# A decoder trunk on eight cores: the gate of the first mixer folded into its output weights on Pool, chunks read a tile later, one weight cast a tile

## What is computed

```python
mod = (c_act @ ada_w[i] + ada_b[i])[:, None, :]          # (B,1,6D)
sh_m, sc_m, gt_m, sh_f, sc_f, gt_f = jnp.split(mod, N_MOD, axis=-1)
h = x * (1 + sc_m) + sh_m
...
return o.reshape(B, S, Q_WIDTH) @ w_o + b_o
...
x = layer_norm(DEEPNORM_ALPHA * x + (1 + gt_m) * y, post_ln_g[i, 0], post_ln_b[i, 0])
```

## Time and profile before

| | |
|---|---|
| time, median of 3 runs | 2449.65 us (2434.49 to 2452.31) |
| the profiled execution | 2451.3 us |
| its span (core 0, the slowest; others 2393.2 to 2442.8) | 2449.9 us |
| busy in the span: PE, DVE, ACT, POOL | 54%, 51%, 26%, 17% |
| software queue: share of the 16 engines, MB | 58.7%, 211.43 |
| hardware queue: share of the 16 engines, MB | 23.6%, 199.60 |
| granted TensorE clock, mean of core 0 | 0.771 |

### The profile page before, as it was taken

How to read it: one execution, slowest core, us unless ns; L and a number is a source line. 1 busy time by engine, 2 the same in 40 slices (tenths; PEclk the granted TensorE clock), 3 DMA queues, 4 the chain that set the end, 5 groups by cost and what they waited for, 6 DMA issues and landing times.

```text
span 2449.9 us, 30623 instructions; the slowest of 8 cores (2393.2 to 2449.9 us)
## 1 busy us (share of the span) xinstructions
PE 1326.5 (54%) x9631; PEld 810.8 (33%) x9631; DVE 1255.0 (51%) x2512; ACT 639.9 (26%) x1251; POOL 427.4 (17%) x558
## 2 busy tenths in 40 slices
PE   1537657766335464255227998989631744557300
PEld 0324434443223343134113443434311533335200
DVE  2344445545345354254218777777523534556388
ACT  1314424544311111012013444444211211112000
POOL 1000002010131111011101221313013211111242
PEclk9768878878667687678658999999965867778655
DMA  9979989985569998799982887879756899999762
GB/s 164 136 129 141 108 105 110 134 98 35 103 111 232 252 223 200 193 215 251 244 170 52 162 163 158 146 144 145 105 129 170 193 263 240 239 248 256 261 216 103
DMA packets 92621, 413.14 MB, mean 169 GB/s; under 512 B 21223, under 2 KB 21223, under 8 KB 80617
## 3 DMA queue, kind: packets, MB, share of 16 engines
q0 software_dynamic: 41344, 211.43, 58.7%
q1 hardware_dynamic: 51102, 199.60, 23.6%
HBM read 454.49 MB, written 165.25 MB: 253 GB/s over the span
## 4 chain that ended last, share of the span: by engine, by line
DMA 44%; PE 21%; DVE 17%; issue 9%; POOL 2%; ACT 2%; another core or an unknown queue 2%; SPq 1%; DVEq 1%; POOLq 0%; ACTq 0%
DMA sb_A<-adaP 7%; DMA sb_W<-wb 7%; DMA sb_x<-xd 6%; PE bank L1354 5%; DMA ys<-sb_hT 3%; DMA ys<-sb_Z 3%; PE bank L1672 2%; DMA sb_W<-ys,sb_idx 2%; DMA sb_A<-post_ln_b 2%; DMA sb_W<-attn_w_qkv 2%; DMA mod<-sb_adfm 2%; DMA sb_hT<-xd 2%; PE bank L1598 2%; DVE sb_hT L1379 2%; PE bank L1629 2%
## 5 line engine op out<-in xcount | busy, mean ns | idle before, releaser
L1354 PE MATMUL bank<-sb_hT,sb_W 128*128 128x256 bf16 x1984 | 308.4, 323 | 165.9 <-DMA sb_W<-wb 133.1
L1354 PEld LDWEIGHTS bank<-sb_hT,sb_W 128*128 128x128 bf16 x1984 | 223.4, 115 | 221.6 <-issue 168.9
L1336 ACT ACTIVATE sb_hT<-bank,sb_H 128x256 bf16<-128x256 f32 x256 | 130.4, 562 | 439.7 <-PE bank L1327 438.7
L1341 DVE TENSOR_SCALAR sb_hT<-bank,sb_H 128x256 bf16<-128x256 f32 x256 | 126.9, 537 | 194.8 <-PE bank L1327 160.1
L1379 DVE TENSOR_TENSOR sb_hT<-bank,sb_gtbf 128x512 f32<-128x512 f32 x176 | 121.5, 691 | 70.0 <-DMA ys<-sb_hT 52.4
L607 POOL TENSOR_TENSOR sb_rstdt<-sb_mvt,sb_eps_t 128x1 f32<-128x1 f32 x64 | 25.6, 401 | 684.6 <-DVE sb_R L445 275.6
L1375 PE MATMUL bank<-sb_W,sb_R 128*128 128x512 bf16 x496 | 132.8, 414 | 12.3 <-DVE sb_hT L1379 10.5
L1598 PE MATMUL bank<-sb_x,sb_Z 128*128 128x512 bf16 x512 | 130.0, 400 | 10.7 <-DVE sb_cact_rep L1653 7.4
L1672 PE MATMUL bank<-sb_W,sb_Z 128*128 128x512 bf16 x512 | 131.7, 404 | 2.2 <-ACT sb_Z L1665 2.2
L1629 PE MATMUL bank<-sb_x,sb_Z 128*128 128x512 bf16 x512 | 121.3, 379 | 0.7 <-issue 0.7
L1316 POOL DMA_INDIRECT sb_hT<-xh,sb_slots x64 | 61.0, 953 | 339.8 <-PE bank L1327 313.8
(11 more groups left out here) (248 smaller groups left out, 2700.5 us busy)
## 6 DMA issues: line engine op xcount, KB each, us to landing
wb<-moe_w POOLq DMA_DIRECT2D x41, 1536.0 KB, 20.6
sb_W<-wb SPq DMA_DIRECT2D x39, 1536.0 KB
ys<-sb_hT SPq DMA_DIRECT2D x44, 1024.0 KB
sb_W<-moe_w POOLq DMA_DIRECT2D x23, 1536.0 KB, 22.9
ys<-sb_Z SPq DMA_DIRECT2D x20, 1024.0 KB
sb_A<-adaP POOLq DMA_DIRECT2D x30, 512.0 KB, 16.3
sb_x<-xin SPq DMA_DIRECT2D x16, 512.0 KB, 11.1
xd<-sb_x SPq DMA_DIRECT2D x16, 512.0 KB, 36.3
```

Source lines behind the costliest of these rows:

```text
L1336: S.op("act", (lambda k=k, src=src: lambda e: e.activation(out=hTe[i][:, k, :], in_=src, func=AF.Identity, scale=H1[haff][:, k:k + 1], bia ...
L1341: S.op("dve", (lambda k=k, src=src: lambda e: e.tensor_scalar(out=hTe[i][:, k, :], in0=src, scalar1=H1[haff][:, k:k + 1], scalar2=H0[haff] ...
L1354: S.op("pe", (lambda k=k, f=f, fc=fc: lambda e: e.matmul(banks[bk][:, f * 256:(f + 1) * 256], wgu[:, k, fc:fc + 128], hTe[i][:, k, :], sta ...
```

## The change

- `CAST[0]` is every odd expert from 5 to 31, 14 of them, where it was 17. `moe_conv(0)` is called once in each iteration from t = 2; it was called once from t = 1 and once more in 3, 5, 7 and 9.
- `mods_rest` is called twice an iteration (after rope and after head group 1); the third call in even iterations is gone. The remainder and `make_aset` move from t = 14 to t = 15.
- Chunks 8 to 11 are consumed at the end of iteration 0, not ahead of the loop; chunks 12 to 19 at the end of iteration 1, not four each in iterations 0 and 1. The loads of x follow them.
- The folds run on Pool, all four in a row from `gate_row`. The bias comes feature-major (`boT`, 128x8); DVE multiplies it with the gate and splits it into two halves, both are stored to new rows 4 and 5 of `mod`, and Pool loads these into rows 0 and 1 of `borow`.

```diff
-        CAST = [[ex for ex in range(4, 32) if ex % 5 in (0, 2, 4)], [ex for ex in range(32) if ex % 4 != 3]]
+        CAST = [[ex for ex in range(4, 32) if ex % 2 == 1], [ex for ex in range(32) if ex % 4 != 3]]
...
+            dma("sp", "dc", boT[:], boT_d, writes=[BboT])
+            S.op("dve", lambda e: e.memset(borow, 0.0), writes=[Bborow])
...
+                def row_store(r, src, bsrc):
+                    S.op("sp", lambda e: e.dma_start(out=mod_d[r].rearrange("(k p) -> p k", p=128), in_=src,
+                                                     allow_slow_non_contiguous=True),
+                         reads=[bsrc], writes=[Bmod[r]], proc="dc")
+
                 def gate_row():
+
                     bc_load(A1, BA1, mod_d[2:3, :], reads=[Bmod[2]])
-                    S.op("dve", lambda e: e.memset(A0[:], 0.0), writes=[BA0])
-                    dma("sp", "dc", A0[0:2, :], bo_d.to_broadcast([2, D]), writes=[BA0])
+                    S.op("dve", lambda e: e.tensor_tensor(out=boT[:], in0=boT[:], in1=adfm[:, 16:24], op=ALU.mult),
+                         reads=[BboT, Badfm[2]], writes=[BboT])
+                    S.op("dve", lambda e: e.tensor_copy(out=bhi16[:], in_=boT[:]), reads=[BboT], writes=[Bbhi])
+                    S.op("dve", lambda e: e.tensor_copy(out=bhi[:], in_=bhi16[:]), reads=[Bbhi], writes=[Bbhi])
+                    S.op("dve", lambda e: e.tensor_tensor(out=boT[:], in0=boT[:], in1=bhi[:], op=ALU.subtract),
+                         reads=[BboT, Bbhi], writes=[BboT])
+                    row_store(4, bhi[:], Bbhi)
+                    row_store(5, boT[:], BboT)
+                    dma("pool", "dw", borow[0:2, :], mod_d[4:6, :], reads=Bmod[4:6], writes=[Bborow])
+                    for k2 in range(4):
+                        fold(k2)
 
                 def fold(k2):
                     w = Wo[:, 2 * k2:2 * k2 + 2, :]
-                    S.op("dve", lambda e: e.tensor_tensor(
+                    S.op("pool", lambda e: e.tensor_tensor(
                         out=w, in0=w, in1=gtrow.unsqueeze(1).to_broadcast([128, 2, D]), op=ALU.mult),
                          reads=[BWo_[k2], Bgtrow], writes=[BWo_[k2]])
-
-                def bias_rows():
...
-                for n in range(8, 12):
-                    early_consume(n, gate_row if n == 11 else None)
-                x_load(6); x_load(7)
...
                         if g == 0:
                             if t >= 1:
                                 Y2a(t - 1)
-                            elif t == 0:
-                                fold(0); fold(1)
                         if g == 1 and job1 is not None:
-                            next(job1, None)
-                        if g == 3 and t % 2 == 0 and job1 is not None:
                             next(job1, None)
...
-                    if t >= 1:
-                        moe_conv(0)
-                    if t in (3, 5, 7, 9):
+                    if t >= 2:
                         moe_conv(0)
...
-                    if t == 0:
-                        fold(2); fold(3)
-                        bias_rows()
...
-                    if t < 2:
-                        for n in range(12 + 4 * t, 16 + 4 * t):
+                    if t == 0:
+                        for n in range(8, 12):
+                            early_consume(n, gate_row if n == 11 else None)
+                        x_load(6); x_load(7)
+                    if t == 1:
+                        for n in range(12, 20):
                             early_consume(n)
-                        for n in range(8 + 4 * t, 12 + 4 * t):
+                        for n in range(8, NT):
                             x_load(n)
...
-                    if t == NT - 2:
+                    if t == NT - 1:
                         for _ in job1:
                             pass
                         make_aset(0, None, None, None)
```

22 lines of the change are left out of this document (7 added, 15 removed).

## The result

The changed kernel takes 2433.24 us (median of 20 runs, 2412.6 to 2459.21), the kernel before 2450.26 in the same comparison (20 runs). The ratio is 0.9909, 95% interval 0.9883 to 0.9934; it leaves out executions in which one die is slower whatever the kernel (7 of the 20 of after; the other 13 have a median of 2430.02). The forecast was 59 us less, the measurement says 17 by all runs and 22 by the ratio. The measured time lies in the upper part of the stated range, to which the prediction gave a chance of 0.19. The direction was right and the tiles became faster for the reason given, but a term that the sum put at 0, `make_aset`, cost 33 us and took back more than half of what the tiles gained. The profiled execution of after has a span of 2418.4 us against 2449.9, both on core 0, each the slowest of its run.

A forecast was written before the change was run, and what follows sets the result against it. The prediction took the attention stage to be held by a gate-row stall and by tiles going as fast as the DMA engines. Its terms, -11 + 2 - 80 + 10 + 20 = -59 us, gave 2392 us, range 2350 to 2442.

The forecast's parts named there:

- make_aset: Tail of the attention stage: moving it from tile 14 to 15 only moves DVE's wait to tile 16; counted 0.
- gate path: Start of the attention stage: store, loads and Pool folds end so that Y2b(0) is done at 173, not 184.0; -11 us.
- eight chunks: End of tile 1: eight chunks consumed there instead of four cost 4 x 0.56 us; +2.
- the pace: Attention tiles: two chunks and one cast each bring 33.0 us a tile down to 26.5, bound by compute; -80 us.
- waits: Attention tiles: not all of PE's instruction waits go, as casts now run until tile 15; 10 us given back.
- The floor: Attention tiles: compute needs near 26 us a tile, 7 under the pace; a tile with no chunk took 25.9.
- Three casts fewer: Expert stage: three more experts load as f32 through Pool, 6.7 us of the engines each; +20 us.
- The gate path is long: Rival, start of attention: both bias stores late, Y2b(0) done at 210, +26 in place of -11, in all 2429; chance 0.10.
- The direct loads cost their whole landing: Rival, expert stage: three f32 loads stand whole on the path, +69 in place of +20, 2441 us; chance 0.10.
- Larger gain: Rival, attention stage: all waits go and folds run at DVE's price, 2359 us; chance 0.12.
- the pace does not fall: Rival, attention tiles: late chunks or slow casts keep every tile at 33.0 us, +25, 2476 us; chance 0.10.

The follow-up runs named there:

- gate_only: The kernel after with before's pace put back (2.5 chunks a tile, 17 casts, chunks drained in tile 14), gate path kept; 0.9995 of before.
- rows_late: The kernel after with the stores of modulation rows 0 and 1 moved behind the load of the expert slots; 0.9885 of before.
- split_after: The kernel after with make_aset's two scaling operations on DVE moved behind the last routing step, its loads left in place; 0.9824 of before.
- casts17: split_rows with before's 17 casts, a second one in tiles 4, 8 and 12; 0.9857 of before.
- split_rows: The kernel after with the edits of rows_late and split_after together; 0.9848 of before.
- pace_only: The kernel before with only two chunks and one cast a tile, 14 casts, chunks drained in tile 15; 0.9973 of before.
- pe_gate_b: pe_gate run again unchanged, on one chip with the kernel after; 2425.37 us, 0.9743 of before.
- aset14: The kernel after with the chunk drain and make_aset's loads put back from tile 15 to tile 14; 0.9877 of before.
- pe_gate: split_rows with gate row and bias rows spread over the partitions by PE instead of stores to DRAM and loads back; 0.9803 of before.

## Why the prediction was wrong in size

Core 0 of the two profiled executions, from the table at the top, beside the terms of the sum:

| stretch | forecast | measured |
|---|---|---|
| to Y2b(1): gate path -11, eight chunks +2, first tile of the pace -3 | -12 | -9 |
| Y2b(1) to Y2b(14): the rest of the pace -77, waits +10 | -67 | -53 |
| Y2b(14) to the first gather: make_aset | 0 | +33 |
| first gather to that of the second layer | +20 | +11 |
| the rest, where nothing was changed | 0 | -14 |
| sum | -59 | -32 |

- **The gate path**: right in its end (Y2b(0) done at 171.1, 173 forecast) by luck, as errors cancel. The gate row landed at 125.3, 9 us before the 134 of the sum; from there the bias rows took 24 us until the folds could start, not 12; the folds took 16.2 us, not 23 (scaling from 128x1 operations overstated Pool; the prediction's other figure, 18, was nearer). But gate_only shows that at before's pace these us are worth nothing; the term counts only with the pace.
- **The pace**: right in kind. PE's wait for `sb_A<-adaP` fell from 50.4 to 14.6 us (over 0 to 660; "under 15"), and what is left of PE's waits is mostly for ACT and DVE. One premise was wrong in its sum: the stretch of 11 tiles had 15 casts and 26 chunks issued in it, not 1.5 and 2.5 a tile, and the queue's own work was 309 us, 28.1 a tile and not 31.3; with the hardware queue that is 29.7, so "32.9 us, the pace itself" agrees with the 33.0 by chance. The term was also mis-sized: 28.1 us a tile where 26.5 was forecast. With the waits that it gave back the sum makes 27.0 a tile; 13 times 1.1 are the 14 us. The floor had been read from a single tile that had no chunks; PE's waits for ACT and DVE were taken as they were in before, 22.5 and 7.3 us in 11 tiles, and were 39.9 and 14.7 in 13.
- **make_aset, "I count 0"**: this is the step that failed: a wait that the sum put at 0 cost 33 us. The prediction looked only at the expert loads. It overlooked the row store ahead of the two rows on SP's queue, though the prediction itself had the price of such a store beside traffic (43.4 us) and used it for the gate only, and it asked what the rows wait for, not who would come to them earlier. All gain of the tiles makes DVE come earlier to make_aset; the rows depend on the last chunk, and that the change had moved later, from 542.1 to 561.5. Y2b(15) hides it: its last product comes 75 us earlier, close to the 79 of the sum, but 13 us of that are DVE's old wait, which stood between Y2b(14) and Y2b(15) and now stands behind both. From there to the first gather the kernel took 39 us and now takes 86. rows_late and split_after, which each remove the wait in a different way, bring the first gather to 634 and 633 from 669, about the 33 us.
- **Three casts fewer**: +20 was right (23 from casts17 to split_rows, 21 from gate_only to pace_only, each pair on one chip). In after it shows as +11 on core 0 and +4 in the median. Why it is less there stays open: pace_only has the same stand of DVE ahead of its stage as after, and shows the whole.
- **The rest**: 14 us less in a part of the program that is the same is the scatter of single executions (the medians over the cores are 560 and 559), and makes most of the difference between 32 us here and the 17 to 22 of the runs.
- **The rivals**: none of the four named this one. *The gate path is long*, 2429, has nearly the measured time, but Y2b(0) was done at 171.1 and not at 210. *The direct loads cost their whole landing*, 2441, is near it too; casts17 excludes it (23 us for three experts, not 69). *Larger gain* would have needed tiles without waits, *the pace does not fall* tiles of 33.0; they took 28.1.

By the middle values the two parts together are worth more than their sum: 0.9995 and 0.9973 alone, 0.9909 in after (the intervals leave room for a plain sum), and with the tail mended 0.982 to 0.989.

The Trainium skill (DMA: Bandwidth & Descriptors, Queues, rings and completion order), which the prediction used for the gate's store, says that an engine goes round the queues packet by packet. The prediction read this as one wait for a packet of the software queue per 4-byte piece; an estimate in that way, with the 1024 pieces spread evenly over 16 engines, 64 each, can be held against the traces. In after on core 1, from 554 to 616, the software queue sent 880 packets in 91.9% of 16 engines' 62 us, 1.04 us a packet: 66 us, and the store landed after 62.1. But in before, from 542 to 569, it sent 79 packets in 116.2% (the shares are rough), 6.4 us a packet: 407 us, and the store landed after 26.8. So one piece a packet is not what the traces show, and the agreement in after proves nothing. They show the landings alone: 16.1 us in an emptying queue, 24.2 to 40.4 beside casts (the last store of before), 62.1 to 67.9 beside a cast and expert loads (the last store of after).

## What to carry to other kernels

When a stretch is made faster, follow each engine to its first wait beyond that stretch, and ask what the awaited data depends on: here the last piece of a side job, which the same change had moved later. Put what nothing needs yet (the scaling of a row, a store for the next layer) behind what is needed, in the engine's order and in the queue's. And an earlier start is worth only what the bound behind it leaves: two edits that alone could not be told from nothing gave 0.9% together.

## What the runs showed of the hardware

- **Four Pool operations in a row held one DVE operation until the last was done.** A DVE operation with two SBUF operands lasted 13.2 to 17.6 us instead of 0.82 beside four Pool operations of 4.05 us, on all sixteen cores of two runs, and ended 0.7 us after the last one, even where its record begins 0.7 us before the first (pe_gate_b, core 1: 128.99 against 129.71). Here the work on Pool hid nothing from a DVE that needed two SBUF operands in that time; no run shows a DVE operation with one. The Trainium skill (SBUF — State Buffer, SBUF: two separate sides) calls the shared port pair an exclusive lock that the loser waits out, held for the whole instruction; that DVE did not get in between the four is more than it says.
- **The same fold, 128x2048 in bf16, is 4.04 us on Pool and 2.22 on DVE**, a ratio of 1.8; the 128x1 operations had suggested 2.5.
- **4 KB stored as 1024 pieces of 4 bytes**: 16.1 us in an emptying queue; beside casts and expert loads 18.7 to 94.5 in before and after, and in after in two groups for one and the same store (18.7 to 27.8 on four cores, 69.5 to 94.5 on the others). What follows on the same queue pays too: an issue that takes 0.32 us held SP for 26.28, one that took 1.52 for 36.84 (aset14), or the load behind it landed after 54 us (pace_only). Spreading the same row over the partitions with PE took from 109.6, when DVE had the column, to 115.9, when ACT had written the second half of the row (pe_gate, core 7), with no transfer at all.
